# Entering a gather stage one tile and one head at a time, with GpSimd making two low parts

## The reference

```python
q = (ht @ w_query).reshape(T, Hh, 2, PEER_HALF)          # 8 heads, 2 halves of 128
scores = jnp.einsum('thpd,hpkd->thpk', q, sub_keys)      # 128 keys per half
s_top, i_top = lax.top_k(scores, K)                      # K = 16
cand = s_top[:, :, 0, :, None] + s_top[:, :, 1, None, :]
best, pos = lax.top_k(cand.reshape(T, Hh, K * K), K)
expert_idx = jnp.take_along_axis(cand_idx, pos, axis=-1)
gates = jax.nn.softmax(best, axis=-1)
# per token and pick (8 heads x 16 picks):
a = gelu(dot(expert_u[idx], x)) * gate
out = sum(a * expert_v[idx])
```

## Time and profile before

| | us |
|---|---|
| median of 3 runs | 2255.34 |
| lowest, highest | 2254.22, 2258.99 |
| profiled execution, first to last instruction (span) | 2253.3 |
| PE busy | 1975.4 (88%) |
| DVE busy | 1561.6 (69%) |
| ACT busy | 1026.2 (46%) |
| POOL busy | 615.9 (27%) |
| DMA moved | 761.24 MB, mean 338 GB/s |

### The profile page before, as it was taken

One profiled execution on the slowest core, in us unless ns is written; L12 is line 12 of the kernel. 1 busy time (PEld: TensorE's weight loads), 2 busy tenths in 40 slices (PEclk: granted clock), 3 DMA queues, 4 the chain that ended last, 5 costly groups with the idle time before them and its releaser, 6 DMA issues. The chain is left out here.

```text
span 2253.3 us, 23976 instructions
## 1 busy us (share of the span) xinstructions
PE 1975.4 (88%) x8056; PEld 1236.1 (55%) x8056; DVE 1561.6 (69%) x2947; ACT 1026.2 (46%) x2165; POOL 615.9 (27%) x551
## 2 busy tenths in 40 slices
PE   5999899878777888899998988888888879999998
PEld 4986666322222333379876634334333326888987
DVE  6977787766667776578877776667777755565554
ACT  4344355444444444445444554444454444544443
POOL 0000045534444444100003544444454440200000
PEclk9999999999999999999999999999999999999999
DMA  8885699999999999886678999999999995343453
GB/s 328 291 340 203 239 419 421 421 421 421 421 421 421 421 421 422 333 329 235 223 269 363 420 422 420 420 421 421 421 416 422 421 421 198 120 150 131 182 192 131
DMA packets 112396, 761.24 MB, mean 338 GB/s; under 512 B 12832, under 2 KB 13600, under 8 KB 26128
## 3 DMA queue, kind: packets, MB, share of 16 engines
q0 software_dynamic: 76480, 548.94, 58.8%
q1 hardware_dynamic: 34832, 207.74, 24.8%
q10 hardware_dynamic: 960, 3.01, 0.4%
HBM read 758.60 MB, written 1.05 MB: 337 GB/s over the span
## 5 line engine op out<-in xcount | busy, mean ns | idle before, releaser
L973 PE MATMUL pair<-uv,p_diag 128*128 128x512 f32 x1352 | 660.1, 622 | 146.2 <-ACT p_diag L2267 145.7
L1655 DVE CUSTOM_DVE_ANT_0 uv<-uv,p_h 128x1024 f32<-128x1024 f32 x338 | 413.7, 1224 | 245.5 <-DMA uv<-in_peer_uv,p_idx 244.0
L554 POOL DMA_INDIRECT uv<-in_peer_uv,p_idx x338 | 387.7, 1147 | 569.2 <-PE pair L973 426.6
L973 PEld LDWEIGHTS pair<-uv,p_diag 128*128 128x128 f32 x1352 | 243.1, 194 | 534.6 <-ACT p_diag L2267 317.0
L1241 DVE TENSOR_TENSOR ring_low<-ring,ring_high 128x2048 fp32r<-128x2048 f32 x144 | 328.8, 2297 | 111.9 <-ACT ring_high L2072 110.8
L2259 ACT ACTIVATE p_act<-p_dot 128x1 f32<-128x1 f32 x512 | 103.3, 202 | 618.1 <-DVE p_dot L1655 616.3
L2072 ACT ACTIVATE ring_high<-ring 128x2048 fp32r<-128x2048 f32 x144 | 271.5, 1908 | 160.1 <-DMA ring<-in_ret_w_in 46.8
L696 PE MATMUL pair<-hT_high,ring_high 128*128 128x256 f32 x960 | 286.9, 299 | 0.1
L696 PE MATMUL pair<-hT_low,ring_high 128*128 128x256 f32 x960 | 272.5, 284 | 0.0
L973 PE MATMUL pair<-uv_high,p_diag 128*128 128x512 f32 x464 | 226.2, 618 | 37.4 <-ACT p_diag L2267 37.2
L696 PE MATMUL pair<-hT_high,ring_low 128*128 128x256 f32 x896 | 254.4, 284 | 0.0
(11 more groups left out here) (401 smaller groups left out, 2719.1 us busy)
## 6 DMA issues: line engine op xcount, KB each, us to landing
ada<-in_ada_w SPq DMA_DIRECT2D x50, 512.0 KB, 5.3
ring<-in_ret_w_in SPq DMA_DIRECT2D x24, 1024.0 KB, 5.5
ring<-in_sgu_w_in SPq DMA_DIRECT2D x24, 1024.0 KB, 6.5
ring<-in_w_up SPq DMA_DIRECT2D x16, 1024.0 KB, 4.8
ring<-in_w_down SPq DMA_DIRECT2D x16, 1024.0 KB, 4.8
mod<-in_ada_w SPq DMA_DIRECT2D x30, 512.0 KB, 5.8
ring<-in_peer_w_query SPq DMA_DIRECT2D x12, 1024.0 KB, 6.4
ring<-in_sgu_w_out SPq DMA_DIRECT2D x12, 1024.0 KB, 4.9
```

The costliest lines, as they stand in the source:

```text
L554: nc.gpsimd.indirect_dma_start(uv_rows[SLOT[l][s]].rearrange("p a d -> p (a d)"), None, experts, bass.IndirectOffsetOnAxis(ap=p_idx[:, k:k ...
L973: mm = nc.tensor.matmul(acc[:, half, :], p_diag[:, n % DIAGS, :], v[:, half * 512:(half + 1) * 512], start=(k == 0), stop=(k == PICKS - 1))
L1655: V.tensor_tensor_reduce(out=u, in0=u, in1=p_h[:, s // PICKS, :], scale=1.0, scalar=0.0, op0=ALU.mult, op1=ALU.add, accum_out=p_dot[:, n % ...
```

## The change

Both entries are rewritten. TensorE first multiplies head 0 for tile 0 alone (`head_tile(0, 0)`), then transposes tile 1, makes the scores of head 0 and tile 0 into a free half of a PSUM pair, and goes on with `head_tile(1, 0)`, `head_tile(0, 1)`, `head_tile(1, 1)`, each 48 matmuls with 128 moving columns. The scores of both heads and both tiles are then made in one go, head 0 of tile 0 a second time. Three of the four warm matmuls after tile 0 go, and the one after tile 1. VectorE searches before it makes tile 1's hT_low and the low parts of blocks 2 and 3 of the query weights; the low parts of blocks 0 and 1 are made by GpSimd (`lows` there, with a semaphore of its own). ScalarE makes the high parts of blocks 0 and 1 earlier (in layer 1 the second one after the first half of the root), copies head 0's tile-0 sum before it takes tile 1's transposes, and copies the rest afterwards.

```diff
+    low_by_pool = [query_first[l] + e for l in range(2) for e in range(2)]
+    low_by_dve = [i for i in range(limit) if i not in low_by_pool]
...
+            def lows(blocks_here):
+
+                for i in blocks_here:
+                    pool.wait_ge(w_high, i + 1)
+                    nc.gpsimd.tensor_tensor(raw_lows[raw_at[i]], raws[raw_at[i]], ring_high[:, high_at[i]].bitcast(F32), ALU.subtract)\
+                        .then_inc(w_low_pool, 1)
...
             modulation_rows(range(2, 8))
+            lows([query_first[0], query_first[0] + 1])
             gathers(0)
...
             modulation_rows(range(9, 12))
+            lows([query_first[1], query_first[1] + 1])
             pool.wait_ge(x_ready, norm_count(3, 1))
...
-                pe.wait_ge(w_low, i + 1)
+                if i in low_by_pool:
+                    pe.wait_ge(w_low_pool, low_by_pool.index(i) + 1)
+                else:
+                    pe.wait_ge(w_low, low_by_dve.index(i) + 1)
...
                 turn_rows(n, p_h, (0,))
-                keep_warm(("query", l, 0), 4)
-                turn_rows(n, p_h, (1,))
                 keep_warm(("query", l, 0), 1)
 
-                def head_product(l, head):
+                def head_tile(head, t, signal=None, used=False):
 
                     name, mat = ("query", l, 0), ("query", l)
-                    if head == 0:
-                        open_sum(name)
                     for kb in range(2):
-                        for t in range(TT):
-                            pe.wait_ge(*taken_small(("hT", n, t, kb)))
+                        pe.wait_ge(*taken_small(("hT", n, t, kb)))
                         high, low = split(first_block_of[mat + (0,)] + kb)
                         for nt in (2 * head, 2 * head + 1):
                             for k in range(BK):
                                 kk = kb * BK + k
-                                n_tile = slice(nt * P, (nt + 1) * P)
+                                n_tile, tokens = slice(nt * P, (nt + 1) * P), slice(t * P, (t + 1) * P)
+                                place = nt % 2 * S + t * P
                                 for j, (a, b) in enumerate(((high, hT[0]), (high, hT[1]), (low, hT[0]))):
-                                    mm = nc.tensor.matmul(sum_of(name)[:, head, nt % 2 * S:(nt % 2 + 1) * S], a[:, k, n_tile], b[:, kk, :],
...
+                                    mm = nc.tensor.matmul(sum_of(name)[:, head, place:place + P], a[:, k, n_tile], b[:, kk, tokens],
...
-                head_product(l, 0)
-                head_scores(l, 0)
-                head_product(l, 1)
-                head_scores(l, 1)
+                head_tile(0, 0, head_ready)
+                turn_rows(n, p_h, (1,))
+                pe.wait_ge(keys_in, 16 * (l + 1))
+                pe.wait_ge(head_taken, l + 1)
+                open_sum(("query", l, 1))
+                head_scores(sum_of(("query", l, 1))[:, 1, :], 0, (0,)).then_inc(first_scores, 1)
+                head_tile(1, 0)
+                head_tile(0, 1)
+                head_tile(1, 1, sum_ready, used=True)
+                pe.wait_ge(*taken_sum(("query", l, 0)))
+                for t in range(TT):
+                    open_small(("scores", l, 0, t))
+                    head_scores(small_of(("scores", l, 0, t)), t, (0, 1)).then_inc(small_ready, 1)
+                pe.wait_ge(first_found, l + 1)
                 columns_product(("query", l, 1), ("query", l), 1, hT)
...
-                    if t == 0:
-                        lows(query_first[n // 2])
+                    if t == 1:
+                        lows_hT(n, ((0, 0), (0, 1)))
                     finish_tile(n, t, h, shift)
...
                 rows_of(0, h8, first_idx_ready, l + 1)
+                lows_hT(1 + 2 * l, ((1, 0), (1, 1)))
+                lows(query_first[l] + 3)
                 dve.wait_ge(*taken_small(name))
...
             def peer(l):
-                n = 1 + 2 * l
-                lows_hT(n, ((1, 0), (1, 1)))
                 first = query_first[l]
-                lows(first + 3)
                 choose_first(l)
...
+                highs(first + 2)
+                act.wait_ge(head_ready, l + 1)
+                did(A.activation(p_qT[:, 0, 0:2, 0:P], head_rows[:, :, 0:P], ACT.Copy), head_taken, l + 1)
+                take_hT(n, ((1, 0), (1, 1)))
                 highs(first + 3)
-                act.wait_ge(head_ready, l + 1)
-                did(A.activation(p_qT[:, 0, 0:2, :].rearrange("p a t -> p (a t)"), sum_of(("query", l, 0))[:, 0, :], ACT.Copy), head_taken, l + 1)
                 act.wait_ge(sum_ready, SUM[("query", l, 0)] + 1)
+                did(A.activation(p_qT[:, 0, 0:2, P:S], head_rows[:, :, P:S], ACT.Copy))
                 did(A.activation(p_qT[:, 0, 2:4, :].rearrange("p a t -> p (a t)"), sum_of(("query", l, 0))[:, 1, :], ACT.Copy),
                     *taken_sum(("query", l, 0)))
```

More of the change, by code:

```diff
@@ L882, in head_product @@
                                 kk = kb * BK + k
[L883 removed]
+                                n_tile, tokens = slice(nt * P, (nt + 1) * P), slice(t * P, (t + 1) * P)
+                                place = nt % 2 * S + t * P
                                 for j, (a, b) in enumerate(((high, hT[0]), (high, hT[1]), (low, hT[0]))):
[L885 to L886 removed]
+                                    mm = nc.tensor.matmul(sum_of(name)[:, head, place:place + P], a[:, k, n_tile], b[:, kk, tokens],
+                                                          start=(t == 0 and kk == 0 and nt % 2 == 0 and j == 0), stop=(kk == KD - 1 and j == 2),
@@ L887, in head_product @@
                                                           skip_group_check=True)
-                        if head and kb == 0:
+                        if used and kb == 0:
                             mm.then_inc(w_used, 1)
[L890 to L901, removed]
+                    if signal is not None:
+                        mm.then_inc(signal, 1)
@@ L902, in head_scores @@
+                def head_scores(rows, t, heads):
+                    for head in heads:
                         for part in range(2):
                             q = 2 * head + part
-                            mm = nc.tensor.matmul(small_of(name)[:, q * P:(q + 1) * P], p_qT[:, 0, q, t * P:(t + 1) * P],
+                            mm = nc.tensor.matmul(rows[:, q * P:(q + 1) * P], p_qT[:, 0, q, t * P:(t + 1) * P],
                                                   p_keysT[:, q, :], start=True, stop=True)
[L906 to L909, removed]
+                    return mm
@@ L1239, in lows @@
                     i = split_blocks[0]
-                    dve.wait_ge(w_high, i + 1)
-                    did(V.tensor_tensor(raw_lows[raw_at[i]], raws[raw_at[i]], ring_high[:, high_at[i]].bitcast(F32), ALU.subtract),
-                        w_low, i + 1)
+                    if i not in low_by_pool:
+                        dve.wait_ge(w_high, i + 1)
+                        did(V.tensor_tensor(raw_lows[raw_at[i]], raws[raw_at[i]], ring_high[:, high_at[i]].bitcast(F32), ALU.subtract),
+                            w_low, low_by_dve.index(i) + 1)
                     split_blocks[0] += 1
@@ L1597, in choose_first @@
                 name = ("scores", l, 0, 0)
-                raw = [small_of(name)[:, p * P:(p + 1) * P] for p in range(2)]
+                raw = [sum_of(("query", l, 1))[:, 1, p * P:(p + 1) * P] for p in range(2)]
                 cand8 = p_cand.rearrange("p a b -> p (a b)")[:, 0:h8 * h8]
```

13 lines of the change are left out of this document (5 added, 8 removed).

## The result

| | before | changed |
|---|---|---|
| median of 4 runs, us | 2256.06 | 2292.95 |
| span of the profiled execution, us | 2253.3 | 2289.1 |
| mean granted clock | 0.982 | 0.975 |

The ratio is 1.0166, 95% interval 1.0154 to 1.0177: 36.9 us slower, where I had predicted 10.6 slower (2266, range 2251 to 2272). The sign was right, and the size was wrong by a factor of three and a half.

A forecast was written before the change was run, and what follows sets the result against it. DMA was taken to bound the gather stages, with TensorE also full early on. Query columns 1 6.2 us later less 0.9 in hand gave +5.3 a layer, +10.6 on 2253.3; the median, 2.0 above the span, became 2266, range 2251 to 2272.

The forecast's parts named there:

- The sign: Whole kernel: slower, given a chance of 0.81, against 0.11 for the same and 0.08 for faster.
- The 128-column step: Head products: a 128-column matmul starts every 0.111 us, paced by its weight load; chance 0.76.
- an earlier first gather gains nothing while query columns 1 come later: Gather stage start: first gather 4.8 us earlier, query columns 1 6.2 later; DMA has only 0.9 us in hand.
- my sum: Both layer entries: query columns 1 6.2 us later less 0.9 in hand, +5.3 a layer, +10.6 in all.
- Cost nothing; without that cover up to 4.8 us a layer.: GpSimd's two low parts per layer, 3.8 to 4.8 us each, end before their first reader and so are hidden.
- lost cover: GpSimd's low parts not hidden by its idling and their late first reader: up to 4.8 us a layer.
- The last sentence of the prediction: Signs of being wrong: matmul step 0.06 or 0.22, gathers from 8 on earlier, or long GpSimd low parts delaying TensorE.
- one more such stretch in each entry would cost up to 1.7 us a layer: Clock rival: another stretch at granted clock 0.50 in each entry, 2269; counted inside the main case's 0.76.
- after similar gaps: Argument against the clock rival: before the first gather, 270 to 272.5 us, the granted clock stands at 1.00.
- my rivals: Columns set the pace 2251 (0.09), two records 2308 (0.06), first gather decides 2246 (0.05), clock 2269 (within 0.76).
- the 0.7 us by which tile 0 was to come earlier: Entry: VectorE starts tile 1's sum at 259.0 instead of 259.72, so tile 0's low-half transposes start 0.7 us earlier.

The follow-up runs named there:

- e3: Kernel before with each 256-column matmul of the head products split into two of 128 columns, nothing moved: 2273.44 us, ratio 1.0080.
- e13: Changed kernel with its four low parts on VectorE, the second ahead of tile 1's norm, and four warm matmuls ahead of the first head product: 2271.40 us.
- e1: Kernel before with only GpSimd making the low parts of each layer's first two query blocks, ScalarE's high parts in changed order: 2271.78 us, ratio 1.0065.
- e4: Changed kernel with four warm matmuls instead of one ahead of the first head product: 2285.32 us, ratio 1.0133.
- e2: Changed kernel with its four GpSimd low parts given back to VectorE: 2275.69 us in the profiled execution, then 2292.98 to 2299.74, ratio 1.0170.
- e5: Changed kernel with low parts back on VectorE and four warm matmuls instead of one: 2275.20, 2277.04, 2298.48 and 2275.11 us, ratio 1.0125.
- e9: Kernel of e3 without the five warm matmuls around the transposes ahead of the head products: 2317.08 us, ratio 1.0256.
- e11: Changed kernel with low parts back on VectorE and twelve warm matmuls instead of one ahead of the first head product: 2282.05 us, ratio 1.0122.
- e6: Changed kernel with its low parts back on VectorE, the same kernel as e2, profiled once more: 2310.95 us.

## Why the prediction was wrong

**Right.** The 128-column step: 0.111 predicted, 0.112 measured (e3). That an earlier first gather gains nothing while query columns 1 come later: in the kernels free of the other losses the time is 2267 to 2270. Their own terms fit too: ScalarE's copy of query columns 1 came 6.2 us later by my sum, and in e13 5.9 in layer 0 and 6.7 in layer 1 more than VectorE was late ahead of each entry. The terms that I had priced thus add up to 11 to 14 us, and I had 10.6. The sign rests on these terms and was no luck.

**The step that failed first:** "Cost nothing; without that cover up to 4.8 us a layer." I costed GpSimd's low parts by GpSimd's own time line (it idles, they end in time), and their own length I had right. But they shut VectorE out for their length, which the earlier trace rows can't show, as a mean of one engine. The changed kernel's low parts met VectorE's two-input instructions just ahead of the entry, where TensorE waits for them. This is 16.1 us (e1; 8.35 + 7.9 in the changed kernel's own profile), above even the price that I had put on lost cover (9.6). The last sentence of the prediction comes near ("low parts over 5 us long with TensorE waiting for them"), but names GpSimd's as those waited for; it was VectorE's.

The profile of before had shown it. GpSimd's group of the earlier trace rows at 1.89 us has this beside it on VectorE (timelines of before, GpSimd, then VectorE):

```profile
1972.37 1.89 POOL L573 TENSOR_TENSOR b_sq<-b_cv 128x1024 f32<-128x1024 f32 x1
```

```profile
1972.74 3.67 DVE L1241 TENSOR_TENSOR ring_low<-ring,ring_high 128x2048 fp32r<-128x2048 f32 x1 [1.11 <-ACT ring_high L2072]
```

VectorE's low part takes about 2.29 everywhere else in before, and 3.67 here: it waits from 1972.74 to GpSimd's end at 1974.26, 1.5 us. I read the duration of the nearest GpSimd row and not what ran beside it.

**The second step that failed:** the clock, "one more such stretch in each entry would cost up to 1.7 us a layer", held unlikely "after similar gaps". The mechanism was among my rivals, its size was not. I took the cost of a low stretch from a row with wide matmuls behind it. Behind this one come 192 narrow matmuls, which in some executions stay at 0.50: 0.213 us each instead of 0.112, up to 20 us a layer. In the changed kernel the stretch is 10 us of layer 0, and four warm matmuls instead of one give 7.6 us back (e4). Removing three warm matmuls was the edit that I had costed at nothing without naming what they held up.

**The account.** 10.6 (my sum) + 16.1 (e1) + 7.6 (e4) = 34.3 of 36.9. The remaining 2.6 are within the error of these terms (e1's alone is 10.6 to 18.5). Layer 0 of the changed kernel's profile adds up on its own: the copy of query columns 1 is 23.6 us late, of which 2.3 were there ahead of the entry, 8.35 are the lock, 4.6 the low clock from 275 to 285, and 1.5 (16.0 - 14.5) the low clock from 301.9 on. That leaves 6.9, where my sum had 6.2: the 0.7 us by which tile 0 was to come earlier did not show. It is not shown why most executions of e2, and one of e5, run so much longer than the others and those of the changed kernel do not. What TensorE must do for the clock to rise was not measured.

## What to carry to other kernels

Work moved to an idle engine is free only if what it shares is idle too: before giving GpSimd a long SBUF instruction, look on VectorE's timeline at what stands beside it, and if it has two SBUF inputs and someone waits for it, add GpSimd's whole length, or cut GpSimd's instruction in pieces (16.1 to 5.6 us here). Halving the moving columns of matmuls whose time is their weight load saves almost nothing on each (0.119 to 0.112 us) and doubles their number; and a low clock ahead of them can last through all of them (e9), so price a low stretch by the matmuls that may run in it. Warm matmuls are worth as many as fill the wait: three too few cost 7.6 us (e4), and twelve instead of four 11 (e11 against e13, which differ in the place of one low part too).

## What the hardware showed

- GpSimd's copy with one input (1.89 us) locks out VectorE's two-input instruction as its subtraction (4.6 us) does; VectorE's instruction with one input in PSUM was not held up beside it (0.68, in layer 1 of e1 and of the changed kernel).
- A gather's issue is held up too: behind a 1.04 us one in the changed kernel the next two take 2.61 and 1.87 beside VectorE's two low parts (290.52 to 295.0), and each ends some 0.8 us behind the end of one of them. After that an issue takes 0.94. That it is the same lock is argued from these times, not tested.
- TensorE was busy 2.50 of 2.50 us in window after window, from 270 to 305 us in e6, at a granted clock of 0.50. All of its matmuls there have 128 columns.
